# The beginning of a one-core two-block network: squares four chunks at a time, first products one chunk behind their modulation, units 2 and 3 of the weights split in other places

## What is computed

```python
mx = jnp.split((jax.nn.silu(c) @ w_mod[l] + b_mod[l])[:, None, :], N_MOD, axis=-1)
mz = jnp.split(jax.nn.silu(c_ctx) @ w_mod[l] + b_mod[l], N_MOD, axis=-1)
x = x + 0.5 * mx[2] * swiglu(modulate(rms_norm(x), mx[0], mx[1]), ffn1_w1[l], ffn1_w3[l], ffn1_w2[l])
z = z + 0.5 * mz[2] * swiglu(modulate(rms_norm(z), mz[0], mz[1]), ffn1_w1[l], ffn1_w3[l], ffn1_w2[l])
# rms_norm(x): x / sqrt(mean(x*x) + 1e-6);  modulate(h, shift, scale): h * (1 + scale) + shift
# swiglu(h, w1, w3, w2): (silu(h @ w1) * (h @ w3)) @ w2, 2816 features wide
```

## Time and profile before

| | us |
|---|---|
| median of 3 runs | 2466.31 (2465.89 to 2467.49) |
| the profiled execution | 2466.78 |
| its span, first to last instruction | 2464.9 |
| TensorE busy | 2396.9 (97%) |
| VectorE busy | 1517.3 (62%) |
| ScalarE busy | 1004.7 (41%) |
| GpSimd busy | 396.6 (16%) |
| mean granted TensorE clock | 0.995 |

### The profile page before, as it was taken

The page is one execution under the profiler, slowest core; times in us unless marked ns, Lnnn a source line. Parts: engine busy times, 40 slices in busy tenths (PEclk is TensorE's granted clock), DMA queues, the critical chain, the costliest instruction groups (busy, mean ns, idle before and its releaser), DMA issues.

```text
span 2464.9 us, 39377 instructions
## 1 busy us (share of the span) xinstructions
PE 2396.9 (97%) x15054; PEld 2101.0 (85%) x15054; DVE 1517.3 (62%) x2554; ACT 1004.7 (41%) x1659; POOL 396.6 (16%) x403
## 2 busy tenths in 40 slices
PE   6999999999999999999999999999999999999998
PEld 4888888667888888888888877999988999989998
DVE  5878765683699865523333575665656665666664
ACT  5222234544522223422223455545445544446443
POOL 2221211240122121111011131121000120000220
PEclk9999999999999999999999999999999999999999
DMA  8556542112266755222223222455433555434553
GB/s 319 201 195 214 179 156 86 60 44 78 90 223 221 252 209 179 86 95 101 96 94 101 79 78 80 164 181 185 163 103 121 171 173 178 154 112 145 190 188 137
DMA packets 97881, 362.50 MB, mean 147 GB/s; under 512 B 11024, under 2 KB 11280, under 8 KB 96560
## 3 DMA queue, kind: packets, MB, share of 16 engines
q1 hardware_dynamic: 75744, 274.42, 32.9%
q0 software_dynamic: 21968, 85.72, 10.0%
HBM read 359.04 MB, written 1.05 MB: 146 GB/s over the span
## 4 chain that ended last, share of the span: by engine, by line
PE 88%; DVE 5%; ACT 4%; issue 2%; DMA 1%; POOL 0%; DVEq 0%; ACTq 0%; SPq 0%; POOLq 0%
PE bank L741 27%; PE bank L743 26%; PE bank L742 26%; ACT ring_high L1230 1%; DVE ring_low L1695 1%; PE bank L1017 1%; PE bank L987 1%; PE bank L1005 1%; PE bank L1039 1%; PE bank L958 0%; PE bank L1180 0%; DVE arena L1761 0%; PE bank L966 0%; PE bank L1095 0%; DVE arena L2031 0%
## 5 line engine op out<-in xcount | busy, mean ns | idle before, releaser
L1695 DVE TENSOR_TENSOR ring_low<-ring,ring_high 128x1024 fp32r<-128x1024 f32 x524 | 650.3, 1241 | 555.3 <-ACT ring_high L1230 553.5
L741 PE MATMUL bank<-x_parts,ring_high 128*128 128x512 f32 (+2 forms) x2700 | 915.9, 339 | 13.2 <-DVE ring_low L1695 11.3
L743 PE MATMUL bank<-x_parts,ring_low 128*128 128x512 f32 (+2 forms) x2700 | 900.7, 334 | 0.0
L742 PE MATMUL bank<-x_parts,ring_high 128*128 128x512 f32 (+2 forms) x2700 | 899.6, 333 | 0.0
L1230 ACT ACTIVATE ring_high<-ring 128x1024 fp32r<-128x1024 f32 x524 | 551.6, 1054 | 632.4 <-PE bank L743 630.9
L741 PEld LDWEIGHTS bank<-x_parts,ring_high 128*128 128x128 f32 x2700 | 510.7, 189 | 89.0 <-issue 25.4
L743 PEld LDWEIGHTS bank<-x_parts,ring_low 128*128 128x128 f32 x2700 | 510.5, 189 | 48.6
L742 PEld LDWEIGHTS bank<-x_parts,ring_high 128*128 128x128 f32 x2700 | 510.8, 189 | 47.1 <-issue 0.5
L604 POOL TENSOR_TENSOR hidden_parts<-fresh,hidden_parts 128x512 fp32r<-128x512 f32 (+2 forms) x132 | 217.4, 1647 | 1361.5 <-ACT hidden_parts L1345 1361.5
L741 PE MATMUL bank<-hidden_parts,ring_high 128*128 128x512 f32 (+2 forms) x1122 | 368.1, 328 | 0.7 <-POOL hidden_parts L604 0.7
L743 PE MATMUL bank<-hidden_parts,ring_low 128*128 128x512 f32 (+2 forms) x1122 | 367.3, 327 | 0.0
(11 more groups left out here) (226 smaller groups left out, 2173.8 us busy)
## 6 DMA issues: line engine op xcount, KB each, us to landing
ring<-stream_dram SPq DMA_DIRECT2D x521, 512.0 KB, 3.3
mod_ring<-w_mod_dram POOLq DMA_DIRECT2D x128, 512.0 KB, 5.0
arena<-w_mod_first_dram POOLq DMA_DIRECT2D x8, 1024.0 KB, 11.4
ring<-stream_dram POOLq DMA_DIRECT2D x3, 512.0 KB, 12.8
arena<-na_bias_dram POOLq DMA_DIRECT2D x2, 768.0 KB, 11.2
mod_ring<-consts_dram POOLq DMA_DIRECT2D x1, 1140.0 KB, 5.4
resid<-x_dram POOLq DMA_DIRECT2D x2, 512.0 KB, 6.0
resid<-ctx_dram POOLq DMA_DIRECT2D x2, 512.0 KB, 9.3
```

What stands on the lines that cost most here:

```text
L741: pe.matmul(out, w[0][:, b], xh, start=start, stop=False)
L742: pe.matmul(out, w[0][:, b], xl, start=False, stop=False)
L743: return pe.matmul(out, w[1][:, b], xh, start=False, stop=stop)
L1695: dve.tensor_tensor(low[:, u % RING], ring[:, u % RING], high_f[:, u % RING], ALU.subtract).then_inc(low_parts, 1)
```

## The change

- Loads: x and ctx first, then chunk 0 of the modulation weights, units 0 and 1, chunks 1 and 2, unit 2, chunk 3, and the others as their slots come free. Before: x, chunk 0, ctx, chunk 1, units 0 and 1, chunk 2, unit 2, chunk 3.
- Squares: ScalarE squares four chunks with one instruction, as soon as their half has landed; VectorE adds 4 + 4, 2 + 2 and 1 + 1 chunks. TensorE takes the mean of x ahead of the first modulation and that of ctx behind the first turn, both into one bank, and one root is taken for all 512 columns.
- Order of products: those of units 0 and 1 with chunk c - 1 come after the turn of chunk c, and unit 2 is taken from chunk 3 on, with chunk c - 3. Five products are left behind the last turn.
- Units: unit 2 is split behind chunk 1 on both engines and no longer behind chunk 2; ScalarE splits unit 3 ahead of the first silu of the feed-forward.
- The silu of the conditioning rows moves behind the silu of gate 1, and the modulation rows of f = 0 are done together with those of f = 1.

```diff
@@ -447,6 +448,10 @@
...
             return scalar2(l, m, c) if isinstance(m, str) else mod[:, l, 0, (m + 1) * KC + c:(m + 1) * KC + c + 1]
+        def c_turn(tag):
+            return 1 if tag == ("ffn1", 0) else 0
...
@@ -651,19 +656,19 @@
...
             half = KC // 2
+            for i in range(2):
+                pool.dma_start(resid[:, i * half:(i + 1) * half, META:META + NX], A["x"][:, i * half:(i + 1) * half]).then_inc(
+                    *made(f"x_loaded{i}", i, by=16))
+            for i in range(2):
+                pool.dma_start(resid[:, i * half:(i + 1) * half, META + NX:META + N1],
+                               A["ctx"][:, i * half:(i + 1) * half]).then_inc(*made(f"ctx_loaded{i}", i, by=16))
             for c in range(KC):
-                if c < 2:
-                    at = META + c * NX
-                    for i in range(2):
-                        pool.dma_start(resid[:, i * half:(i + 1) * half, at:at + NX],
-                                       A["ctx" if c else "x"][:, i * half:(i + 1) * half]).then_inc(
-                                           *made(f"ctx_loaded{i}" if c else f"x_loaded{i}", i, by=16))
-                for s in ((), (), (0, 1), (2,))[c] if c < 4 else ():
-                    pool.dma_start(ring[:, s], A["stream"][s]).then_inc(*made(f"first_unit_loaded{s}", s, by=16))
                 if c >= FIRST_SLOTS:
...
                     *made(f"first_mod_loaded{c % FIRST_SLOTS}", c, by=16))
+                for s in ((0, 1), (), (2,))[c] if c < 3 else ():
+                    pool.dma_start(ring[:, s], A["stream"][s]).then_inc(*made(f"first_unit_loaded{s}", s, by=16))
             pool.dma_start(resid[:, :, 0:META], A["meta"]).then_inc(*made("meta_loaded", 0, by=16))
...
@@ -813,21 +818,25 @@
...
+                means = take("mean", ("start",))
+                pe.wait_ge(*when("consts_loaded", 0))
+                pe.wait_ge(*when("first_sums", 0))
+                pe.matmul(means[:, 0:NX], cst(C_ONESD), sumsq[:, 0:NX], start=True, stop=True)
                 pe.wait_ge(*when("c_cols_silu", 0))
-                for c in range(KC):
+                first_modulation(0)
+                first_turn(0)
+                pe.wait_ge(*when("first_sums", 1))
+                pe.matmul(means[:, NX:N1], cst(C_ONESD), sumsq[:, NX:N1], start=True, stop=True).then_inc(
+                    *made("mean", ("start",)))
+                for c in range(1, KC):
                     first_modulation(c)
-                    if c == 0:
-                        pe.wait_ge(*when("consts_loaded", 0))
-                    if c < 2:
-                        mean_square(("start",), c)
-                    if c >= 4:
-                        part(2, c - 4)
+                    if c >= 3:
+                        part(2, c - 3)
                     first_turn(c)
-                    if c >= 2:
-                        part(0, c - 2)
-                        part(1, c - 2)
+                    part(0, c - 1)
+                    part(1, c - 1)
                 pe.wait_ge(*when("consts_loaded_rest", 0))
-                for i, c in ((0, 6), (1, 6), (2, 4), (2, 5), (0, 7), (1, 7), (2, 6), (2, 7)):
+                for i, c in ((2, 5), (0, 7), (1, 7), (2, 6), (2, 7)):
                     part(i, c)
...
@@ -1317,6 +1326,8 @@
...
                 nf = FC // parts
+                if tag == ("ffn1", 0):
+                    split_ahead(1)
                 for h in range(parts):
...
@@ -1335,11 +1346,13 @@
...
                                     *made("silu", tag, h, f, frees=("gate", tag, h, f)))
-                            if tag == ("ffn2", 0) and h == 0 and f == 0:
+                            if tag in (("ffn1", 0), ("ffn2", 0)) and h == 0 and f == c_turn(tag):
+                                l = 0 if tag[0] == "ffn1" else 1
                                 for s in range(2):
-                                    act.wait_ge(*when("c_ctx_loaded" if s else "c_loaded", 1))
-                                    act.activation(csilu[:, s], csilu[:, s], ACT.Silu).then_inc(*made("c_silu", 1, s))
-                            split_ahead(1)
+                                    act.wait_ge(*when("c_ctx_loaded" if s else "c_loaded", l))
+                                    act.activation(csilu[:, s], csilu[:, s], ACT.Silu).then_inc(*made("c_silu", l, s))
+                            if tag != ("ffn1", 0) or h or f:
+                                split_ahead(1)
                         if f >= 1:
...
@@ -1627,25 +1640,25 @@
...
             act.wait_ge(*when("eps_one", 1))
+            half = KC // 2
             for g in range(2):
-                for d in range(KC):
-                    square(("start",), d, g, f"ctx_loaded{d // 4}" if g else f"x_loaded{d // 4}", d // 4)
-                first_rows(g)
-                if g == 1:
-                    split_ahead(1 - RING)
-                root_of_mean(("start",), g)
+                a, b = norm_cols(("start",), g)
+                for i in range(2):
+                    act.wait_ge(*when(f"ctx_loaded{i}" if g else f"x_loaded{i}", i))
+                    c = slice(i * half, (i + 1) * half)
+                    act.activation(scaled[:, c, a:b], resid[:, c, META + a:META + b], ACT.Square).then_inc(
+                        *made("first_squares", g, i))
+            first_rows(0)
+            split_ahead(1 - RING)
+            act.wait_ge(*when("mean", ("start",)))
+            inverse_root(rstd[:, 0], bank("mean", ("start",)), N1, ("start",), ("mean", ("start",)))
             first_high(0)
             split_ahead(1)
-            first_high(1)
-            first_rows(2)
-            split_ahead(1)
-            first_high(2)
-            for c in range(3, KC):
+            for c in range(1, KC):
                 first_rows(c)
                 first_high(c)
-            for s in range(2):
-                act.wait_ge(*when("c_ctx_loaded" if s else "c_loaded", 0))
-                act.activation(csilu[:, s], csilu[:, s], ACT.Silu).then_inc(*made("c_silu", 0, s))
+                if c == 1:
+                    split_ahead(1)
             for l in range(DEPTH):
...
@@ -1789,6 +1802,8 @@
...
                     todo = list(mod_chunks(l, h, g)) if l is not None else []
+                    if l is not None and h == 0 and g <= c_turn(tag):
+                        todo = list(itertools.chain(*(mod_chunks(l, h, i) for i in range(g + 1)))) if g == c_turn(tag) else []
                     for j in todo[:len(todo) // 2]:
...
@@ -2275,7 +2290,7 @@
...
                     a, b = norm_cols(("start",), g)
-                    dve.wait_ge(*when("rstd", (("start",), g)))
+                    dve.wait_ge(*when("rstd", ("start",)))
                     dve.scalar_tensor_tensor(scaled[:, c, a:b], resid[:, c, META + a:META + b],
...
@@ -2292,25 +2307,28 @@
...
             for g in range(2):
-                for d in range(KC):
-                    sum_squares(("start",), d, g)
-                if g == 0:
-                    dve.wait_ge(*when("small_loaded", 0))
-                first_shift_scale(g)
+                a, b = norm_cols(("start",), g)
+                dve.wait_ge(*when("first_squares", g, 1))
+                dve.tensor_tensor(scaled[:, 0:4, a:b], scaled[:, 0:4, a:b], scaled[:, 4:8, a:b], ALU.add).then_inc(
+                    *made("first_fours", g))
+                dve.wait_ge(*when("first_fours", g))
+                dve.tensor_tensor(scaled[:, 0:2, a:b], scaled[:, 0:2, a:b], scaled[:, 2:4, a:b], ALU.add).then_inc(
+                    *made("first_twos", g))
+                dve.wait_ge(*when("first_twos", g))
+                dve.tensor_tensor(sumsq[:, a:b], scaled[:, 0, a:b], scaled[:, 1, a:b], ALU.add).then_inc(
+                    *made("first_sums", g))
+            dve.wait_ge(*when("small_loaded", 0))
+            first_shift_scale(0)
             split_ahead(1 - RING)
...
             split_ahead(1)
-            first_scaled(1)
-            first_low(1)
-            first_shift_scale(2)
-            first_scaled(2)
-            split_ahead(1)
-            first_low(2)
-            for c in range(3, KC):
+            for c in range(1, KC):
                 first_shift_scale(c)
...
                 first_low(c)
+                if c == 1:
+                    split_ahead(1)
             for l in range(DEPTH):
...
```

3 lines of the change are left out of this document (2 added, 1 removed).

## The result

| | us |
|---|---|
| changed kernel, median of 10 runs | 2462.07 (2460.05 to 2466.86) |
| kernel before, median of 10 runs beside it | 2467.04 (2463.74 to 2471.34) |
| ratio, 95% interval | 0.9982 (0.9974 to 0.9990) |
| profiled execution of the changed kernel | 2463.61, span 2461.1 |

A forecast was written before the change was run, and what follows sets the result against it. TensorE, busy 2396.9 of 2464.9 us, was taken as the bound, so only the beginning could give time. Starting unit 3 at 53.2 instead of 57.84 saves 4.6 us: 2462.2 profiled, 2461.7 beside the median, range 2459.6 to 2463.8.

The forecast's parts named there:

- Loads, squares, sums: At the start: chunk 0 lands at 13.8, a loss of 2.7 us; squares and sums are hidden, up to 0.1 us.
- To the turn of chunk 1: First scaling starts at 19.8 instead of 22.85, turn of chunk 1 at 22.7, set by ScalarE's order.
- To the modulation of chunk 7: Modulation of chunk 7 starts at 45.5 instead of 47.39, TensorE's order being the bound at 3.74 us per chunk.
- The end: After the last modulation: products end at 52.7; TensorE starts unit 3 at 53.2, after a wait of 0.5 us.
- one of the signs by which it called itself wrong: In the chunk steps: a chunk's low part coming after its turn in the queue would make the prediction wrong.
- The sum: Whole beginning: 57.84 - 53.2 = 4.6 us saved, giving 2462.2 us profiled, 2461.7 beside the median.
- fewer products: Behind the last turn: five products stand there instead of eight, 2.04 us less.
- 0.7 to unit 3: At unit 3's split, moved ahead on ScalarE: TensorE waits 0.5 us in place of 1.2.
- The clock as uncertain term: TensorE's rate rises 3.7 to 5.2 us after it becomes continuously busy, the same distance as before.
- the later clock: In the beginning: rate rises one chunk later, losing 1.6 us; with the later-load case, 2463.1 us, chance 0.15.
- The slower one: Loads of chunks 6 and 7 land late and delay unit 3: 1.8 us slower, 2468.2 us, chance 0.03.
- The one by which products one chunk behind buy nothing: Chunk steps: the chain of vector work, not TensorE's order, paces them; gain 2.3 us, 2464.0 us, chance 0.05.

The follow-up runs named there:

- e1: Changed kernel with the loads in their old order; first product with unit 3 starts at 54.44 us, against 53.96 in the changed kernel.
- e2: Changed kernel with squares and sums one chunk at a time, as before; first product with unit 3 starts at 53.99 us against 53.96.
- e10: Changed kernel with the product of unit 2 and chunk 6 ahead of unit 0 and chunk 7; first product with unit 3 at 53.98 us.
- e4: Changed kernel with unit 3's split, conditioning silus and one f = 0 modulation row as before; median 2466.29 us, ratio to kernel before 1.000.
- e3: Changed kernel with products two chunks behind and eight behind the last turn, as before; median 2465.54 us, ratio to kernel before 0.9993.
- e6: Kernel before with only the part on unit 3 and the conditioning rows changed; median 2464.71 us, ratio to kernel before 0.9994.
- e7: Changed kernel plus 20 unused matmuls on constants ahead of the mean of x; median 2459.73 us, ratio to kernel before 0.9973.
- e8: Changed kernel plus unused matmuls: 20 before x's mean, 5 after ctx's mean, 2 after chunk 1's modulation; median 2460.28 us, ratio to kernel before 0.9978.

## Why the prediction was right, and where it missed

**Loads, squares, sums: right.** Chunk 0 at 13.67 (13.8 forecast), mean of x before it, sums hidden. e1 puts the order of loads at 0.3 to 0.5 us, no more than the scatter, and e2 the size of the squares at nothing in U. The reason that the prediction gave for the earlier scaling, that the squares of ctx no longer stand behind the first root in ScalarE's queue, fits the rows (the earlier trace rows has the mean of ctx wait for its sum until 19.55, the changed kernel takes it at 16.97 without a wait), but no run undid that order alone. With it and the loads turned, even single squares end in time. The landing of chunk 7, 37.1 by the prediction, came at 39.0 (asked for at 32.1, 6.9 us later); unit 3 was asked for at 39.3 and took 7.0 us, to 46.3, still 5 us ahead of its use.

**To the turn of chunk 1: right.** Scaling 19.67 (19.8), turn 22.51 (22.7), paced by ScalarE as said.

**To the modulation of chunk 7: right, in part by luck.** It starts at 45.65 (45.5), since two errors go against each other. The turn of chunk 1 was 0.2 early, and the clock rose later than I took: the modulation of chunk 2 took 1.94 and not 1.55, and that of chunk 3 followed 4.53 after it and not 4.18. TensorE's order paces the chunks there, 3.71 to 3.76 us apart.

**The end: one step failed.** The prediction checked that a low part is ready in time with the cover of a full step, 3.4 us. For the last chunk there is no next modulation: behind its turn stand the two products of chunk 6 and one of chunk 5, about 2.0 us, and the low part needs 2.5. By the products alone the last one of gate 0 would have begun 4.33 after the modulation, at 49.98, just as forecast; it began at 50.54, 0.56 later, of which the trace has 0.41 as a wait (ends of matmuls are modelled), and gate 0 is done so much later. The prediction had put this wait at nothing, and a low part that comes after its turn in the queue is one of the signs by which it called itself wrong: here it came, for one chunk of eight. It is that product that needs the low part of chunk 7, so another order of whole products gives nothing back, as e10 shows for one. Whether its first matmul, which reads only the high part, could go ahead of the wait was not tried. Products and unit 3: 0.41 wait for unit 3 (0.5 forecast), U = 53.96 (53.2).

**The sum.** 3.9 us in the profiled executions against 4.6; the difference is that 0.56 and 0.15 at the modulation of chunk 7. The runs gave 4.4 by the ratio. That this lies nearer to the forecast than the traces do is luck: its interval is 3.9 us wide, the moment of the clock and what lies behind U scatter, and half a microsecond outside the span, which the prediction doesn't have, goes the other way.

**How it was split was less right than the total.** The prediction put 2.0 us to fewer products and 0.7 to unit 3. The table above has 0.7 for unit 3 alone, as forecast, but 0.1 for fewer products alone and 1.4 with the part on unit 3 in place (9.70 and 9.75 to 8.31): that figure hardly exists without the other part, and the wait for chunk 7 takes 0.6 off it.

**The clock as uncertain term: right to name, its size too small.** I took one distance, with 1.5 us to either side. Over the executions without added matmuls the last rise came from the modulation that began at 26.15 (e4) to past 36.7 (e3), 4 to 10 us after TensorE had become busy. The page "TensorE: Matmul & The Clock Gate" of the Trainium skill, section "Part 1: The HAM clock gate", says that the moment moves from run to run; these traces agree, and show more of it than the single trace of before could.

**The rivals.** None of them came as a whole; of the later clock there were 0.4 us in one modulation. The slower one needed a landing more than 15.7 us after the issue; chunk 7 had 6.9. The one by which products one chunk behind buy nothing had 2.3 us; e3 and the estimate there give them 1.6 on top of the rest. Behind U nothing happened: VectorE's three modulation rows and ScalarE's line ran beside 270 us of products without a wait.

## What to carry to other kernels

A start-up in which every engine has its own fixed order could be forecast here to within a microsecond in 54 by placing each step behind the latest of its waits; the places to check one by one are the last turns of a loop, where the cover of a full turn is missing. Two edits at one chain need not be worth the sum of what each is worth alone (here 2.1 us against 0.8), so undo them singly and together. Where runs scatter by more than the gain, measure from the trace between two events that enclose nothing else.

## What the runs showed of the hardware

- The moment at which TensorE's rate (1.2 or 2.4 GHz) rose differs much between executions of nearly the same program. Counted from the turn behind which TensorE was busy with hardly a gap, it came 4.0 us later in e4 and in e10, 4.8 in the kernel before, about 6 in the changed one, 10 in e3. In e6 it first rose only 2.9 us after the very first matmul (11.17), although the kernel before has the same rows there and stayed at the lower rate, with 0.85 for the turn of chunk 0 and 1.93 for the modulation of chunk 1:

```profile
14.05 0.55 PE L797 MATMUL bank<-const,fresh 128*128 128x2 f32 x4
16.41 1.07 PE L788 MATMUL bank<-arena,act_out 128*32 128x256 f32 x16 [1.80 <-DMA arena<-w_mod_first_dram]
19.59 1.22 PE L749 MATMUL bank<-sumsq,const 128*128 128x256 f32 x2 [2.11 <-DVE sumsq L1737]
```

- It also falls in one execution and not in another. In e6 it fell near 17.5, as the modulation of chunk 1 ended, so that the mean (1.22) and the modulation of chunk 2 (1.94) went at the lower rate. In e7 it fell near 14.7, inside a modulation, after waits of 1.74 and 1.16 us with 0.70 us of work between them; in e8, with waits of 1.67 and 1.19 at the same places, it stayed high. One execution of a kernel doesn't tell what the next will do there.
- The granted clock of a stretch was 1.00 in the kernel before and in the changed one while modulations took 1.94 us, the lower rate. Here is the changed kernel from 15 to 60 us, with 1.00 in spite of two such modulations:

```profile
15.00:60.00 45.00, 40.69 (x253) 26.80 (x246) 25.07 (x60) 22.36 (x39) 8.93 (x16) 1.00 0.91 348
```

Only in e6 and e7, where the rate had been high and fell, does the column show the lower rate (0.81 from 15 to 60 us in both, 0.50 in stretches that lie wholly in it). Up to the first fall it is the length of like matmuls that tells the rate.
